# Paired bodies of a decoder-layer kernel: the block products copied and folded at units 34 and 35, the turned keys split at unit 33

## The reference

```python
h = _rmsnorm(x, norm_g[l])
proj = h @ w_in[l]
qa, ka, va, za, qb, kb, vb, zb, fb, qm, zm, gl = _split_cols(proj, IN_WIDTHS)
...
oa = _dilated_mixture(qa, ka, va, rel_bias)        # 12 heads of 128
ua = (oa * jax.nn.silu(za)) @ w_proj_a[l]
...
ob = _forgetting_attention(qb, kb, vb, log_f)      # 8 heads of 128
ub = (ob * jax.nn.silu(zb)) @ w_proj_b[l]
...
om = _memory_attention(qm, km, vm)                 # 4 heads of 256, into 256 memory tokens
um = (om * jax.nn.silu(zm)) @ w_proj_m[l]
g = jax.nn.sigmoid(gl.reshape(B, S, N_BRANCH, D_MODEL) + b_gate[l])
merged = g[:, :, 0] * ua + g[:, :, 1] * ub + g[:, :, 2] * um
x = x + (merged @ w_out[l]).astype(x.dtype)
```

## Time and profile before

| | us |
|---|---|
| median of three runs | 1165.74 |
| lowest and highest | 1164.64, 1166.91 |
| the profiled execution | 1162.97 |
| its span in the trace | 1161.2 |
| TensorE busy (PE) | 1150.1, 99% |
| TensorE weight loads (PEld) | 952.5, 82% |
| VectorE busy (DVE) | 875.7, 75% |
| ScalarE busy (ACT) | 593.2, 51% |
| DMA, mean over the span | 238 GB/s |

### The profile page before, as it was taken

How to read it: one execution, slowest core, us unless ns; L and a number is a source line. 1 busy time by engine, 2 the same in 40 slices (tenths; PEclk the granted TensorE clock), 3 DMA queues, 4 the chain that set the end, 5 groups by cost and what they waited for, 6 DMA issues and landing times.

```text
span 1161.2 us, 13866 instructions
## 1 busy us (share of the span) xinstructions
PE 1150.1 (99%) x5235; PEld 952.5 (82%) x5235; DVE 875.7 (75%) x1112; ACT 593.2 (51%) x736; POOL 44.3 (4%) x37
## 2 busy tenths in 40 slices
PE   8999999999999999999999999999999999999998
PEld 7788888888888888788788788888888888888887
DVE  6776588576667569778777866789769858988997
ACT  6565445445545545635554553545535544554643
POOL 1110000000010000000000000000000000000000
PEclk9999999999999999999999999999999999999999
DMA  9998789658577687687678686655865685485872
GB/s 336 315 274 305 255 267 330 218 188 288 188 241 255 208 271 254 208 262 231 241 236 262 225 271 212 220 175 186 290 208 181 224 266 166 168 290 181 270 245 101
DMA packets 148049, 276.12 MB, mean 238 GB/s; under 512 B 9805, under 2 KB 33029, under 8 KB 147984
## 3 DMA queue, kind: packets, MB, share of 16 engines
q1 hardware_dynamic: 135904, 258.31, 66.6%
q10 hardware_dynamic: 11600, 16.87, 4.8%
q0 software_dynamic: 480, 0.07, 0.0%
HBM read 251.34 MB, written 26.24 MB: 239 GB/s over the span
## 4 chain that ended last, share of the span: by engine, by line
PE 95%; DVE 2%; DMA 1%; ACT 1%; issue 0%; SPq 0%; ACTq 0%
PE acc L1865 22%; PE acc L1873 22%; PE acc L1869 22%; PE acc L2060 4%; PE acc L2062 4%; PE acc L2056 4%; PE side L2031 2%; PE side L2033 2%; PE side L2028 2%; PE acc L2031 1%; PE acc L2033 1%; PE acc L2028 1%; DVE w_lo L1569 1%; PE side L2060 1%; PE side L2062 1%; PE side L2056 1%
## 5 line engine op out<-in xcount | busy, mean ns | idle before, releaser
L1177 DVE TENSOR_TENSOR w_lo<-w_raw,w_hi 128x1024 fp32r<-128x1024 f32 x213 | 258.6, 1220 | 144.0 <-ACT w_hi L752 143.4
L752 ACT ACTIVATE w_hi<-w_raw 128x1024 fp32r<-128x1024 f32 x213 | 224.6, 1059 | 234.2 <-PE acc L1873 215.7
L1569 DVE TENSOR_TENSOR w_lo<-w_raw,w_hi 128x1024 fp32r<-128x1024 f32 x170 | 206.7, 1219 | 71.4 <-ACT w_hi L996 71.0
L996 ACT ACTIVATE w_hi<-w_raw 128x1024 fp32r<-128x1024 f32 x170 | 178.4, 1056 | 136.0 <-PE acc L1873 102.2
L1865 PE MATMUL acc<-w_hi,hT_hi 128*128 128x512 f32 x764 | 205.8, 391 | 0.0
L1869 PE MATMUL acc<-w_lo,hT_hi 128*128 128x512 f32 x764 | 204.3, 389 | 0.0
L1873 PE MATMUL acc<-w_hi,hT_lo 128*128 128x512 f32 x764 | 204.3, 389 | 0.0
L1869 PEld LDWEIGHTS acc<-w_lo,hT_hi 128*128 128x128 f32 x764 | 143.4, 188 | 30.0
L1873 PEld LDWEIGHTS acc<-w_hi,hT_lo 128*128 128x128 f32 x764 | 143.4, 188 | 29.9
L1865 PEld LDWEIGHTS acc<-w_hi,hT_hi 128*128 128x128 f32 x764 | 142.1, 188 | 29.4 <-issue 0.9
L996 ACT ACTIVATE w_hi<-group 128x1024 fp32r<-128x1024 f32 x48 | 50.8, 1060 | 60.2 <-PE acc L2062 48.4
(11 more groups left out here) (286 smaller groups left out, 1485.9 us busy)
## 6 DMA issues: line engine op xcount, KB each, us to landing
w_raw<-in_w_in_dram SPq DMA_DIRECT2D x124, 1024.0 KB, 6.0
w_raw<-in_w_in_dram SPq DMA_DIRECT2D x39, 512.0 KB, 4.8
w_raw<-in_w_mem_kv_dram SPq DMA_DIRECT2D x16, 1024.0 KB, 6.0
w_raw<-in_w_proj_a_dram SPq DMA_DIRECT2D x12, 1024.0 KB, 7.9
w_raw<-in_w_proj_m_dram SPq DMA_DIRECT2D x8, 1024.0 KB, 8.5
w_raw<-in_w_proj_b_dram SPq DMA_DIRECT2D x8, 1024.0 KB, 5.1
w_raw<-in_w_out_dram SPq DMA_DIRECT2D x16, 512.0 KB, 5.0
w_raw<-in_w_out_dram SPq DMA_DIRECT2D x8, 1024.0 KB, 6.2
```

The lines of the kernel that those rows point to most:

```text
L752: act.activation(whi[:, ring(u0, s)], raw[:, slot, UK * (s % 2):UK * (s % 2) + UK], ACT.Copy)\
L996: act.activation(whi[:, at], source, ACT.Copy).then_inc(hi_done, 1)
L1177: dve.tensor_tensor(wlo[:, ring(u0, s)], raw[:, (l0 + s // 2) % RING, UK * (s % 2):UK * (s % 2) + UK], whi[:, ring(u0, s)].bitcast(F32), A ...
L1569: dve.tensor_tensor(wlo[:, at], source, whi[:, at].bitcast(F32), ALU.subtract).then_inc(lo_done, 1)
```

## The change

Two tables of constants and the places that read them. `U_PRODUCTS` had three entries, of which ScalarE used the first two and VectorE the last two; now it has two, which both use. ScalarE's copies go from units 32 and 33 to 34 and 35, VectorE's folding from 33 and 34 to 34 and 35. The split of the turned keys is made at unit 33 in paired bodies, on both engines; in the other bodies it stays at 29. No instruction is added or removed.

```diff
-U_PRODUCTS, U_PAIRED_BIAS = (32, 33, 34), 33
+U_PRODUCTS, U_PAIRED_KSPLIT, U_PAIRED_BIAS = (34, 35), 33, 33
@@ ScalarE, split_late
-                if s == U_KSPLIT:
+                if s == (U_PAIRED_KSPLIT if paired(g) else U_KSPLIT):
                     act.wait_ge(kT_in, 16 * g + 16)
@@ VectorE, values_folded
-                if s == U_PRODUCTS[1]:
+                if s == U_PRODUCTS[0]:
                     dve.wait_ge(first_copied, 2 * n + 1)
...
-                if s == U_PRODUCTS[2]:
+                if s == U_PRODUCTS[1]:
                     dve.wait_ge(oz_lo, 2 * g)
```

## The result

The changed kernel takes 1155.13 us, the median of five runs (1154.16 to 1155.25). The kernel before takes 1164.64 us beside it (five runs, 1164.06 to 1166.91). The ratio is 0.9911, with a 95% interval of 0.9897 to 0.9926: 0.9% faster, 9.5 us. Forecast were 7.4 us and 1158.3, with a range from 1155.3, so the gain was larger than I said, and the time lies 0.2 us outside the range.

What follows compares the result with a forecast made beforehand. TensorE was taken to bound the kernel, busy 1150.1 of 1161.2 us. Copies and folding 5.91 plus split 1.51 made 7.42 us off the median 1165.74, so 1158.32, range 1155.3 to 1160.9.

Steps and rivals of the forecast that it cites:

- TensorE bounds the kernel, and only its gaps count: Whole span: TensorE busy 1150.1 of 1161.2 us at full clock; other engines' work matters only through TensorE's idle time.
- ScalarE's copies cost 1.97 us a body, 5.91 in all: Unit 33 to the next unit 0 in three paired bodies: copies delay `w_hi`; moving copies and folding gains 5.91 us.
- The lead of ScalarE and VectorE, 34 and 35: Ends of paired bodies: `w_hi` of 34 over 4 us early, second half of v done 3.4 us before unit 0.
- The split of the keys, 1.51 us: Body 5's block product: moving the split from 29 to 33 gives back 1.51 us, 0 in bodies 4 and 6.
- The rival that gave more: Gather stalling in two or three bodies, one or two times 1.51 us more: 1156.8 or 1155.3; chance 0.12.
- The median carried over: Profiled execution lay 2.77 us below the three runs' median; that difference kept, so 1165.74 - 7.42 = 1158.32.
- The bias DMA: Unit 33 on ScalarE: leaves near 463.3 instead of 468.77; price 0, about 10 us of cover for weight loads.
- Slower: Next body's unit 0 waits for VectorE's second half of v; 6.8 us late loses 2.8 in all, 1168.5; chance 0.03.

Runs made afterwards that it cites:

- third trace of before: The kernel before, unchanged, run once more for another trace of it: 1165.40 us.

## Why the prediction was off, step by step

- **TensorE bounds the kernel, and only its gaps count.** Right for the kernel before. With the gaps gone the span is what the matmuls take, in every variant without them. Two kernels in between also lost time to the clock, which the prediction did not price.
- **ScalarE's copies cost 1.97 us a body, 5.91 in all.** Right, mechanism and size: 5.80 between the two kernels without the wait for the gather.
- **The lead of ScalarE and VectorE, 34 and 35.** Right to a few tenths: `w_hi` of 34 at T - 0.5 (forecast T - 0.4 to T - 0.1), the split at T - 1.5 (forecast T - 1.6), the end of v 3.55 us before unit 0 (forecast 3.4).
- **The split of the keys, 1.51 us.** This term of the sum failed. The mechanism was right (`w_hi` of units 30 and 31 queued behind a wait for a DMA), its size was not: 3.9 us on average, and 1.5, 2.8 and 4.2 in three traces. I took the value of one execution, though that execution lay 1.67 us below the fastest run, and the term is the only one in the sum that hangs on a DMA's landing. The rows had the means to do better: body 4 waited 2.36 us for nothing and body 5 waited 4.48 for a loss of 1.51, so body 4 had about 0.6 us of cover left. The rival that gave more had the right account but 0.12 of chance, and it priced each late body at 1.51 where 2.07 occurs. With 3.9 for the term the sum is 9.8. The three pairs of medians taken side by side gave 9.5, 9.9 and 11.1 us (the last 1165.89 and 1154.79), so the term is 3.6 to 5.2 by these differences.
- **The median carried over.** The three runs of before had 1165.74, the five beside the result 1164.64. The time came out 3.2 us under the forecast: 2.1 of it is the gain, the term above, and 1.1 is this shift of the starting value, which nothing in the change explains.
- **The bias DMA.** It left at 461.29, T - 2.1, not T - 0.5: its row stands inside the two `w_hi` before the split, so ScalarE issued it before the split had run. What it waited for was VectorE's `w_lo` of unit 31 (`lo_done`, a wait in the code that the prediction left out): in all bodies of the three traces of the full change it leaves 0.07 to 0.16 us after that has ended (461.22 here). With only the copies moved `w_lo` of 31 ended at 464.78 in body 4, and the DMA left at 464.86. As forecast, it cost nothing. By the Trainium skill ("DMA: Bandwidth & Descriptors", Queues, rings and completion order) queues with work take turns, so a weight load should be slower beside it. The two landing times that the prediction set side by side (6.0 and 5.7 us) fit that but don't show it. In body 4 of the changed kernel the load issued while the bias DMA was in flight landed after 6.7 us and the next three after 4.9 to 5.2; in its two other traces it is 5.7 against 4.9 to 5.1. That agrees, but an earlier load was in flight too, so how much of it is the bias DMA isn't shown. It made no difference to the time.
- **Slower.** The mechanism of this rival did not occur: v ended 3.55 us before unit 0. The split alone does cost time (+1.2 us), but by another way, which the prediction did not have: with the copies left where they were it stands between the third copy and `w_hi` of 34, and delays that.

Not settled: why the writes of the turned keys land later in one execution than in another. No run varied its DMAs.

## What to carry to other kernels

An instruction that waits for a DMA stalls whatever is queued behind it on its engine. Put it as late as the landing needs and its consumer allows (here two units later was enough, and more gave nothing), and count a lead in time, not in units, where the units are short. The price of such a wait read from one trace is one sample. Work out its cover, the wait less the loss (here 4.48 - 1.51, 3.0 us): bodies that wait nearly as long and lose nothing (here 2.4 us) may lose in another execution, and where the traced one is faster than the runs beside it, that is the term to enlarge first. Two moves on one in-order engine must be priced together: here one half gave 6.2 us, the other lost 1.2, and both gave 9.9.

## What the runs showed that I had not expected

- Two waits of 0.99 us within 2.7 us, after a busy stretch, were followed by 3.8 us at a mean granted clock of 0.55, which cost another 1.6 us. Nearly the same pair, 0.92 and 0.99 us, in body 5 of the third trace of before left it at 1.00, and so did the 1.97 us at the end of each body of before. Two runs of the kernel before, its slowest on one chip (1168.41 and 1168.98), have a mean clock of 0.998 where its traces have 1.000, so the clock probably falls in some of its executions too. What decides isn't shown by these runs.
- A DMA issue in ScalarE's list can leave before the engine's instruction ahead of it has started: at 461.29, with the split, ahead of it in the list, at 461.91. With the copies at 33 and 34, it left at 463.95, inside the copy at 463.75. A wait ahead of it in the list does hold it: in the kernel before it left at 468.77, just after the third copy had got VectorE's sum and started, at 468.69.
